# Two dense layers computed as seven half-size block products in place of eight

## What is computed

```python
def _sq_relu_mlp(h, w1, w2):
    a = jax.nn.relu(h @ w1)
    return (a * a) @ w2
...
        x = x + _sq_relu_mlp(_rmsnorm(x, g_mlp[l]), w1[l], w2[l])
    return _rmsnorm(x, g_final)
```

## Time and profile before

| | us |
|---|---|
| median of 3 runs | 2529.43 |
| lowest, highest | 2523.27, 2533.08 |
| the profiled execution (its span) | 2534.1 |
| busy in it: TensorE, VectorE, ScalarE, GpSimd | 2480.9, 1100.9, 770.4, 725.0 |

### The profile page before, as it was taken

One profiled execution on the slowest core, in us unless ns is written; L12 is line 12 of the kernel. 1 busy time (PEld: TensorE's weight loads), 2 busy tenths in 40 slices (PEclk: granted clock), 3 DMA queues, 4 the chain that ended last, 5 costly groups with the idle time before them and its releaser, 6 DMA issues.

```text
span 2534.1 us, 33500 instructions
## 1 busy us (share of the span) xinstructions
PE 2480.9 (98%) x12476; PEld 2073.8 (82%) x12476; DVE 1100.9 (43%) x1795; ACT 770.4 (30%) x1332; POOL 725.0 (29%) x464
## 2 busy tenths in 40 slices
PE   7999999999999999999999999999999999999998
PEld 3888878887888888888888888877888888888886
DVE  5756536466465445444455644344421121120224
ACT  4443434343124434434444412232210020110110
POOL 1323222222572222222222233212332333332331
PEclk9999999999999999999999999999999999999999
DMA  9413022224442222122221343112211111111112
GB/s 319 147 53 108 28 95 65 84 69 138 146 160 88 80 68 84 49 73 75 71 69 53 137 174 127 39 59 75 75 42 50 50 50 46 45 50 50 50 50 75
DMA packets 56422, 213.00 MB, mean 84 GB/s; under 512 B 7912, under 2 KB 8168, under 8 KB 51312
## 3 DMA queue, kind: packets, MB, share of 16 engines
q1 hardware_dynamic: 34448, 126.82, 14.8%
q10 hardware_dynamic: 21856, 84.55, 10.3%
HBM read 168.85 MB, written 28.87 MB: 78 GB/s over the span
## 4 chain that ended last, share of the span: by engine, by line
PE 92%; DVE 5%; DMA 1%; ACT 1%; issue 1%; POOL 0%; SPq 0%; DVEq 0%; ACTq 0%; POOLq 0%
PE ps L2248 13%; PE ps L2250 13%; PE ps L2252 13%; PE ps L2232 12%; PE ps L2234 12%; PE ps L2233 12%; PE ps L2701 3%; PE ps L2510 1%; PE ps L2486 1%; PE ps L2798 1%; PE ps L2822 1%; DMA ada<-in_w_ada_dram 1%; PE ps L2847 1%; PE ps L2851 1%; PE ps L2848 1%
## 5 line engine op out<-in xcount | busy, mean ns | idle before, releaser
L481 POOL CAST w_hi<-raw 128x1024 fp32r<-128x1024 f32 x176 | 187.8, 1067 | 1537.0 <-issue 603.2
L2232 PE MATMUL ps<-act_hi,w_hi 128*128 128x512 f32 x1248 | 500.3, 401 | 2.3 <-DVE act_lo L2096 1.1
L2234 PE MATMUL ps<-act_hi,w_lo 128*128 128x512 f32 x1248 | 489.9, 393 | 0.0
L2233 PE MATMUL ps<-act_lo,w_hi 128*128 128x512 f32 x1248 | 488.4, 391 | 0.0
L483 POOL TENSOR_TENSOR w_lo<-raw,w_hi 128x1024 fp32r<-128x1024 f32 x176 | 432.2, 2456 | 14.1
L2248 PE MATMUL ps<-act_hi,w_hi 128*128 128x512 f32 x896 | 351.2, 392 | 6.0 <-DVE act_lo L1399 4.0
L2250 PE MATMUL ps<-act_lo,w_hi 128*128 128x512 f32 x896 | 350.1, 391 | 0.0
L2234 PEld LDWEIGHTS ps<-act_hi,w_lo 128*128 128x128 f32 x1248 | 235.1, 188 | 52.0
L2252 PE MATMUL ps<-act_hi,w_lo 128*128 128x512 f32 x896 | 277.0, 390 | 0.0
L2232 PEld LDWEIGHTS ps<-act_hi,w_hi 128*128 128x128 f32 x1248 | 235.5, 189 | 46.6 <-DVE vct L1563 2.4
L2233 PEld LDWEIGHTS ps<-act_lo,w_hi 128*128 128x128 f32 x1248 | 235.8, 189 | 41.0
(11 more groups left out here) (426 smaller groups left out, 3862.2 us busy)
## 6 DMA issues: line engine op xcount, KB each, us to landing
raw<-in_w_stream_dram SPq DMA_DIRECT2D x192, 512.0 KB, 3.3
ada<-in_w_ada_dram SPq DMA_DIRECT2D x4, 2048.0 KB, 18.0
spill<-res ACTq DMA_DIRECT2D x16, 512.0 KB, 5.0
gate_dram<-gate_sb ACTq DMA_DIRECT2D x32, 256.0 KB, 2.0
stage<-spill ACTq DMA_DIRECT2D x16, 512.0 KB, 4.0
rope_sb<-in_rope_dram ACTq DMA_DIRECT2D x4, 1024.0 KB, 5.1
stage<-in_x_t_dram ACTq DMA_DIRECT2D x8, 512.0 KB, 4.4
mkv_dram<-mkv_out ACTq DMA_DIRECT2D x4, 1024.0 KB, 4.2
```

The source lines that it names most:

```text
L481: nc.gpsimd.tensor_copy(w_hi[:, s, :, :], raw[:, s, :, :]).then_inc(S["w_hi"], 1)
L2232: nc.tensor.matmul(out, wh, xh, start=start, stop=False)
L2233: nc.tensor.matmul(out, wh, xl, start=False, stop=False)
L2234: return nc.tensor.matmul(out, wl, xh, start=False, stop=stop)
```

## The change

Both layers are computed by the Winograd form of Strassen's scheme on 2x2 blocks: seven products of half-size blocks in place of eight, for some additions of blocks. Both operands' blocks are summed before they are split into high and low, so all sums are made anew in float32.

*Phase 1, hidden layer.* A pair is 256 hidden features (two weight tiles), n = 0 to 15. The four quarters of a pair's weights (128 features by 512 inputs) give seven operands, and x3 by halves of features and tokens gives seven (`X_HI`, `X_LO`, kept in SBUF for all pairs). Product i is 4 k x 3 = 12 matmuls into one bank; `PLACE` says which of the pair's four. Products 4, 5 and 6 add onto a bank that products 1, 3 and 0 have filled, after it has been read. `pair_weights(n)` on GpSimd makes four sums (`summed` 0, 2, 6, 3) and the low parts (`low` 0 to 6); ScalarE makes the high parts (`w_high(n, i)`, for 0, 2, 3, 6 from the sum). Operand i has one slot for all pairs, free once product i of the pair before is done, and `raw` holds one pair, reloaded after `low` 4 and `low` 5. VectorE reads the banks (`evacuate` steps 0 to 5), makes z22, z11, z21, z12 with relu, ScalarE squares them; `turned` makes the three sums and the difference that the second layer needs; seven 128x512 pieces go to DRAM (`a_dram`), three by `plain_kept`, four by `turned_kept`.

*Phase 2, output layer.* 32 tiles m (n = 16 + m), in eight chunks q of 512 hidden features, four tiles each. The chunk's seven operands of the relu's values come back from DRAM (`set_load`), ScalarE and VectorE split them (`set_high`, `set_low`, 128x1024). A product is 2 k x 3 = 6 matmuls, a tile 42. The weights' slots are halved and used in turn. VectorE adds each product to `res` or to a sum `au`. In the last chunk the final norm's squares are added on the way.

The wom tiles now come in the order 0, 4, 1, 5, ..., so that x3's upper and lower rows end in pairs, and its blocks' sums are made between them (`x_sum`, `x_high`, `x_low`). Loops over tiles are written out.

```diff
+PAIRS = 16
+CHUNKS = 8
...
+        PLACE = [3, 0, 1, 2, 0, 2, 3]
...
+        W_SUMS = {True: [0, 2, 3, 6], False: [0, 2, 6, 3]}
+        W_LOWS = {True: [1, 0, 3, 2, 4, 5, 6], False: [1, 0, 2, 3, 4, 5, 6]}
...
+        a_dram = nc.dram_tensor("a_dram", [PAIRS, P, 7, BANK], F).ap()
...
+            def mlp_tile(idx, low):
+                sp.wait_ge(S["wv_lo"], LEFT["wv_lo"] + low)
...
+            for n in range(1, PAIRS):
+                mlp_tile(w_tile(n, 0), w_low_count(n - 1, 4))
+                mlp_tile(w_tile(n, 1), w_low_count(n - 1, 5))
...
+            def set_load(q, j):
...
+                if j == 0:
+                    sp.wait_ge(S["kept_z"], 32 * (2 * q + 2))
+                    sp.wait_ge(S["kept_t"], 48 * (2 * q + 2))
+                sp.dma_start(SETS[7 * (q % 2) + j][2].rearrange("p (k c) -> p k c", k=2),
+                             a_dram[2 * q:2 * q + 2, :, j, :].rearrange("k p c -> p k c")
+                             ).then_inc(S[f"set_in{j}"], 16)
...
-            split_range(T_MLP + 2, 62)
+            def pair_weights(n):
+                a11, a12, a21, a22 = (w_raw(n, o, h) for o in range(2) for h in range(2))
...
+                free = 7 * (min(n, PAIRS) - 1 if n < PAIRS + 2 else n - 2)
+                def summed(i, out, x, y, op):
+                    nc.gpsimd.tensor_tensor(out, x, y, op).then_inc(S["wv_sum"], 1)
+                    pool.wait_ge(S["wv_sum"], LEFT["wv_sum"] + w_sum_count(n, i))
+                def low(i, whole):
+                    pool.wait_ge(S["wv_hi"], LEFT["wv_hi"] + 7 * n + i + 1)
+                    nc.gpsimd.tensor_tensor(lo[i], whole, hi[i].bitcast(F), ALU.subtract).then_inc(S["wv_lo"], 1)
...
+                if n:
+                    pool.wait_ge(S["wv_done"], LEFT["wv_done"] + free + 1)
+                summed(0, s1, a21, a22, ALU.add)
+                low(1, a11)
+                if n:
+                    pool.wait_ge(S["wv_done"], LEFT["wv_done"] + free + 3)
+                else:
+                    pool.wait_ge(S["tile_done"], T_MLP - 1)
+                summed(2, s2, s1, a11, ALU.subtract)
+                if n:
+                    if n == 1:
+                        pool.wait_ge(S["ss_ready"], NORM["x3"] + 1)
+                    if n >= PAIRS:
+                        pool.wait_ge(S["wv_done"], LEFT["wv_done"] + free + 7)
+                    else:
+                        pool.wait_ge(S["wv_lo"], LEFT["wv_lo"] + 7 * n)
+                    summed(6, late, s2, a12, ALU.subtract)
+                low(0, s1)
+                if n:
+                    pool.wait_ge(S["wv_done"], LEFT["wv_done"] + free + 4)
+                summed(3, s3, a21, a11, ALU.subtract)
+                if not n:
+                    low(3, s3)
+                    pool.wait_ge(S["tile_done"], T_MLP)
+                    summed(6, late, s2, a12, ALU.subtract)
+                low(2, s2)
+                if n:
+                    low(3, s3)
+                low(4, a12)
+                low(5, a22)
+                low(6, late)
...
+            def first_product(n):
+                act.wait_ge(S["wv_done"], LEFT["wv_done"] + 7 * n + 2)
+                if n:
+                    act.wait_ge(S["ev_read"], LEFT["ev_read"] + 5 * n)
+                nc.scalar.activation(u_sum, bank(base(n)), ACT.Copy).then_inc(S["u_copied"], 1)
...
+            def turned_kept(n):
+                act.wait_ge(S["a_turn"], LEFT["a_turn"] + 4 * n + 4)
...
+            def set_high(q, j):
+                hi, _, whole = SETS[7 * (q % 2) + j]
+                act.wait_ge(S[f"set_in{j}"], LEFT[f"set_in{j}"] + 16 * (q + 1))
+                nc.scalar.activation(hi, whole, ACT.Copy).then_inc(S["set_hi"], 1)
+            for n in range(PAIRS):
+                w_high(n + 1, 0)
+                if n:
+                    turned_kept(n - 1)
+                    first_product(n)
+                w_high(n + 1, 1)
+                if n == PAIRS - 1:
+                    set_high(0, 0)
+                    set_high(0, 1)
+                w_high(n + 1, 2)
+                if n == 0:
+                    act.wait_ge(S["rstd_spread"], NORM["x3"])
+                    nc.scalar.activation(sp3, ps[:, 0:2 * BANK], ACT.Copy).then_inc(S["rstd_copied"], 1)
+                w_high(n + 1, 3)
+                if n == PAIRS - 1:
+                    set_high(0, 2)
+                    set_high(0, 3)
+                squared(n, 0)
+                w_high(n + 1, 4)
+                squared(n, 1)
+                if n == PAIRS - 1:
+                    set_high(0, 4)
+                w_high(n + 1, 5)
+                squared(n, 2)
+                plain_kept(n)
+                if n == PAIRS - 1:
+                    set_high(0, 5)
+                    set_high(0, 6)
+                w_high(n + 1, 6)
+                squared(n, 3)
+            turned_kept(PAIRS - 1)
...
+            def evacuate(n, step):
+                b0 = base(n)
+                done, at = S["wv_done"], LEFT["wv_done"] + 7 * n
+                if step == 0:
+                    dve.wait_ge(done, at + 3)
+                    dve.wait_ge(S["u_copied"], LEFT["u_copied"] + n + 1)
+                    nc.vector.tensor_tensor(u_sum, bank(b0 + 1), u_sum, ALU.add).then_inc(S["ev_read"], 1)
+                elif step == 1:
+                    dve.wait_ge(done, at + 4)
+                    dve.wait_ge(S["ev_read"], LEFT["ev_read"] + 5 * n + 1)
+                    nc.vector.tensor_tensor(t_sum, bank(b0 + 2), u_sum, ALU.add).then_inc(S["ev_read"], 1)
+                elif step == 2:
+                    dve.wait_ge(S["ev_read"], LEFT["ev_read"] + 5 * n + 2)
+                    dve.wait_ge(S["kept_z"], 32 * n)
+                    if n == 0:
+                        dve.wait_ge(S["rstd_copied"], 1)
+                    nc.vector.tensor_tensor(z22, t_sum, bank(b0 + 3), ALU.subtract).then_inc(S["ev_read"], 1)
+                    relu(n, z22, z22, 5 * n + 3)
+                elif step == 3:
+                    dve.wait_ge(done, at + 5)
+                    nc.vector.scalar_tensor_tensor(out=z11, in0=bank(b0), scalar=0.0, in1=sp3[:, 0:BANK], op0=ALU.max,
+                                                   op1=ALU.mult).then_inc(S["a_relu"], 1)
+                elif step == 4:
+                    dve.wait_ge(done, at + 6)
+                    nc.vector.tensor_tensor(z21, u_sum, bank(b0 + 2), ALU.add).then_inc(S["ev_read"], 1)
+                    relu(n, z21, z21, 5 * n + 4)
+                else:
+                    dve.wait_ge(done, at + 7)
+                    dve.wait_ge(S["kept_t"], 48 * n)
...
+            def turned(n):
+                dve.wait_ge(S["a_sq"], 4 * n + 4)
+                nc.vector.tensor_tensor(turn1, z11, z12, ALU.subtract).then_inc(S["a_turn"], 1)
+                dve.wait_ge(S["a_turn"], LEFT["a_turn"] + 4 * n + 1)
+                nc.vector.tensor_tensor(turn2, z22, turn1, ALU.add).then_inc(S["a_turn"], 1)
+                dve.wait_ge(S["a_turn"], LEFT["a_turn"] + 4 * n + 2)
+                nc.vector.tensor_tensor(z12, z11, turn2, ALU.subtract).then_inc(S["a_turn"], 1)
+                nc.vector.tensor_tensor(turn4, z21, turn2, ALU.subtract).then_inc(S["a_turn"], 1)
+            def set_low(q, j):
+                hi, lo, whole = SETS[7 * (q % 2) + j]
+                dve.wait_ge(S["set_hi"], LEFT["set_hi"] + 7 * q + j + 1)
+                nc.vector.tensor_tensor(lo, whole, hi.bitcast(F), ALU.subtract).then_inc(S["set_lo"], 1)
...
+            n = PAIRS - 1
+            evacuate(n, 0)
+            set_low(0, 0)
+            set_low(0, 1)
+            evacuate(n, 1)
+            evacuate(n, 2)
+            set_low(0, 2)
+            evacuate(n, 3)
+            set_low(0, 3)
+            set_low(0, 4)
+            evacuate(n, 4)
+            set_low(0, 5)
+            evacuate(n, 5)
+            turned(n)
+            set_low(0, 6)
...
+                if m == 0:
+                    dve.wait_ge(S["kept_t"], 48 * PAIRS)
+                    dve.wait_ge(S["kept_z"], 32 * PAIRS)
+                    nc.vector.memset(acc3[:, :], 0.0)
...
+                elif q + 1 < CHUNKS:
+                    set_low(q + 1, SETS_AT[o][0])
+                dve.wait_ge(done, at + 5)
+                nc.vector.tensor_tensor(r11, r11, bank(b0), ALU.add).then_inc(S["ev_read"], 1)
...
+                if not final and o < 3:
+                    set_low(q + 1, SETS_AT[o][1])
+                if final and o:
+                    add_final(2 * o - 1)
+                    add_final(2 * o - 2)
...
+            def hidden_product(n, i, ready=None):
+                pe.wait_ge(S["wv_lo"], LEFT["wv_lo"] + w_ready_count(n, i))
...
+                elif i >= 4:
+                    pe.wait_ge(S["ev_read"], LEFT["ev_read"] + 5 * n + i - 3)
+                product(n, i, range(4), lambda k: x_part(X_HI, i, k), lambda k: x_part(X_LO, i, k), ready
+                        ).then_inc(S["wv_done"], 1)
...
+            for i in range(7):
```

(10 more changed lines are left out.)

566 lines of the change are left out of this document (391 added, 175 removed).

## The result

The changed kernel is slower: 2581.19 us median (2577.81 to 2585.98, 4 runs) against 2527.3 us of the kernel before on the same chip, a ratio of 1.0212 with a 95% interval of 1.0186 to 1.0238. That is 54 us more, where 8.6 us less was predicted; it lies outside the range (2492 to 2547), and in the case (worse than 2550) that the prediction had given a chance of 0.03.

What follows compares the result with a forecast made beforehand. TensorE alone was taken to bound the kernel before. Terms -86.9 + 22.7 + 23.3 - 2.9 + 21.2 + 7 + 7 = -8.6 us took the 2529.4 us median to 2521, range 2492 to 2547.

Steps and rivals of the forecast that it cites:

- What goes: Both layers: 3072 matmuls become 2688, and 384 fewer at 0.2264 us each save 86.9 us.
- Prices: New work: GpSimd 1.30 us on 512 columns, 0.75 on 256; VectorE collisions cost GpSimd about 0.55 or 1.05 us.
- Hidden layer: Steady state: a weight cycle through three engines takes 20.8 us a pair against TensorE's 19.0, costing +22.7 us.
- DRAM traffic I cost at nothing: Whole change: a chunk's sets and tiles, 5.6 MB in 38 us (150 GB/s), were given no cost.
- First transition: Into the hidden layer: idle before the squares' sums (9 us) and product 6, plus lower clock, +23.3 us.
- Second transition: Hidden to second layer: product 4 of tile 16 comes 18.3 us late, plus 2.9 for the clock, +21.2 us.
- Second layer: Output layer: GpSimd 9.9 us a tile against 9.5, mostly absorbed, +3 us; last four tiles +4 us.
- 7 lows and 4 sums, 8.1, and set_low 1.8: Second layer: GpSimd's own operations (8.1 us) and time lost to set_low (1.8 us) make 9.9 us a tile.
- The lead of 8 us: Second layer: a lead of 8 us absorbs nearly all of the 11 us that 28 tiles fall behind.
- Tail: After the last big matmul: late last evacuation, three half squares and a cold spread, 22 instead of 15 us, +7.
- 2: Second layer: GpSimd and set_low together pass TensorE, at 0.82 us per 256 columns; 2549 us, chance 0.20.
- Rivals 1 and 3: 1: cycles close, hidden pairs at 19 us, 2498, chance 0.20. 3: TensorE stays bound, transitions overlap better, 2467, chance 0.07.

Runs made afterwards that it cites:

- e5: Changed kernel with the three turned stores issued behind w_high(n + 1, 1), no longer before the copy of product 1: 2562.13 us.
- e9: e2 with the plain stores (z22, z11, z21) issued an iteration later, behind the landing of the raw tiles: 2538.12 us.
- e2: Changed kernel with w_high(n + 1, 1) first in ScalarE's queue in the hidden layer, before w_high(n + 1, 0), stores and copy: 2553.27 us.
- e13: Changed kernel without GpSimd's unread old splits of the hidden layer's first two tiles: 2574.31 us.
- e6: Changed kernel, second transition: tile 16's sum 6 to w_late, acc3's memset and waits two tiles on, set_high 5, 6 and set_low 5 later: 2569.95 us.
- e1: Changed kernel with w_high(n, 1) before w_high(n, 0) in ScalarE's queue in the second layer: 2551.35 us.
- e12: e11 with the copy of product 1 put before the five stores in ScalarE's queue in the hidden layer: 2497.16 us.
- e14: e12 with e13's one line, the old splits of two tiles taken out: 2496.28 us, ratio 0.9860 to the kernel before.
- e11: e8 plus plain stores behind the raw tiles' landing and pair 15's turned sums and stores behind tile 16's first evacuations: 2514.42 us.
- e8: Changed kernel with the edits of e1, e2, e6 and e7 (ScalarE's copy of the spread moved forward in the first transition): 2512.67 us.

## Why the prediction was wrong

Point by point, by its own steps.

- *What goes*: right. The profile after has 12092 matmuls, and products run at 0.2264 us.
- *Prices*: right. GpSimd 1.28 to 1.30 us on 512 columns, 0.74 on 256; a collision 0.99 us on 1024 (forecast 1.05), and 0.33 to 0.5 on 512 (1.62 to 1.79 in place of 1.29; forecast 0.55).
- *Hidden layer*: the cycle's engines and the place of the wait (product 4, released by the copy) were right; two links were mis-sized. The three issues were priced at 0.34 us each, from the smaller stores of gate_dram, and took 0.38, 0.49 and 0.84; moved away, they give 1.4 us a pair (e5). The reload was priced at 3.5 us, from single tiles that land in 3.3, and took 4.9 in the mean. With no store near it (e9) it still took 4.6, so about 1 us a pair is the two tiles' own and 0.3 us the stores beside them: "DRAM traffic I cost at nothing" was a small error in this kernel, and became one of 1.5 us a pair only with e2's order. Low 1 to low 5 came out shorter, 12.8 us for 13.5. So pairs took 22.1 us in the mean, where I had 20.8: 17 us over the 13 pairs. The rest of the miss is the count: I had given the cycle 2.5 us of lead and 13 pairs. It had no lead (pair 1 took 20.4 us, pair 2 23.3), and 15 pairs paid. +22.7 became +46.3.
- *First transition*: the failed step took product 0 as following the last wom tile at once; it came 10.03 us late. The step left out GpSimd's old splits in front of sum 0. Without them (e13) the rest of this step is right within 0.1 us. +23.3 became +33.9.
- *Second transition*: right, +21.2 and +22.4. e6 shows the chain as a whole, not each of its links.
- *Second layer*: the failed step is the sum "7 lows and 4 sums, 8.1, and set_low 1.8". Both terms were right, and the third, 0.96 us in each tile for w_high 1 behind w_high 0, was missing. I had that link in the hidden cycle and not here. It made GpSimd's 9.9 us a tile into 10.75 (11.0 in tiles with two parts), so that 28 tiles fell behind by 28 x 1.24 = 35 us where I had 11. The lead of 8 us was there and was absorbed, as forecast: tiles m = 1 to 6 ran at 9.5 us, and the 28 tiles lost 26 us. The last four lost 7 in place of 4. +7 became +33.0, and e1 took 27.5 of it away.
- *Tail*: right, +7.5; no run tested it (22.4 to 22.9 us in all).
- *Rivals*: 2 named the place (GpSimd and set_low pass TensorE in the second layer) and the sign, but with a dearer operation as its cause; the operation cost what I had forecast. Rivals 1 and 3 are excluded for this kernel. e12 comes near to 1's condition, pairs at 19 us, but by moves in the code.

Of the 62 us between forecast and time, the three steps explain 60. The gains of single edits don't add: e1, e2, e6 and e13 alone give 88 us by the length, and e14, with e9's, e11's and e12's moves besides, gives 89. By the stretches the missing gain is where a stretch starts earlier and meets its supplier's lead used up: pair 1 and pair 15 in the hidden layer, and the second layer from m = 2 on.

## What to carry to other kernels

Where an engine is to become nearly full, write its cycle down as a list of starts, with each wait for another engine's *queue position* in it, in every stage anew: here a 0.42 us copy in the wrong order cost 0.96 us in each of 28 tiles. Price a transfer that closes a cycle as it is issued, here as two tiles together (4.6 us) and not as one (3.3), and ask before an issue is moved what else starts in the same microsecond (6.1 us). Split every run at the same few starts: a gain that comes back in the next stretch is invisible in the total. And when a stage is replaced, look for loops outside the diff whose bounds still reach into it.

## What the runs showed of the hardware

- In the hidden layer of the changed kernel the clock fell after some of the short waits before product 4, and their length does not tell which. After 2.44 us of idle at 1896.21 the matmuls came every 0.43 us from 1897.37 on, the lower of TensorE's two levels (1.2 GHz); after 2.44 us at 2052.51 they kept following each other 0.23 us apart. Of 15 waits of 0.8 to 2.7 us seven were followed by the lower level, the shortest of them 1.82 us:

```profile
1896.21 0.47 PE L2714 MATMUL ps<-act_hi,w_hi 128*128 128x512 f32 x1 [2.44 <-DVE sq L2540]
...
1897.37 0.63 PE L2715 MATMUL ps<-act_lo,w_hi 128*128 128x512 f32 x1
...
2052.51 0.47 PE L2714 MATMUL ps<-act_hi,w_hi 128*128 128x512 f32 x1 [2.44 <-DVE sq L2540]
2052.81 0.39 PE L2715 MATMUL ps<-act_lo,w_hi 128*128 128x512 f32 x1
```

  Each fall cost TensorE some 1.7 us. What of it reached the time is not shown: the rows of the cycle above name GpSimd, ScalarE and the reload.
- The profiled executions reach the block at two times. In those of the kernel before, e5, e8 and e11 TensorE waits twice at about 343 us, for some 5 us in all and with nothing in the profile that it waits for, and the anchor starts at 1804.5 to 1806.3. In the ten others these waits are absent and the anchor starts at 1792.8 to 1796.7. The cause stays open. The rows are e11's:

```profile
343.05 0.27 PE L2861 MATMUL ps<-con,res 128*128 128x2 f32 x1 [1.97 <-issue]
346.40 3.36 PE L2861 MATMUL ps<-con,res 128*128 128x2 f32 x15 [3.08 <-issue]
```
